# A hybrid attention/mLSTM layer step: the second head's scores moved next to the first head's transposes, and the first head's weighted values moved next to the second head's transposes

## What is computed

```python
q = (rmsnorm(cq_raw) @ w_q_up).reshape(B, T, 16, 128 + 64)      # per head: q_nope, q_pe
kv = (ckv @ w_kv_up).reshape(B, S, 16, 128 + 128)               # per head: k_nope, v
s = (q_nope . k_nope + q_pe . k_pe) * ATTN_SCALE                # scores
p = softmax(where(mask, s, -inf))                               # float32
out = p . v
```

## Time and profile before

| | us |
|---|---|
| median of 3 runs (lowest to highest) | 1999.95 (1999.67 to 2000.25) |
| the profiled execution | 1999.66 |
| its span, first to last instruction | 1997.9 |
| PE busy in the span | 1988.2 |
| DVE, ACT, POOL busy | 1211.7, 909.5, 192.3 |

### The profile page before, as it was taken

The page is one execution under the profiler, slowest core; times in us unless marked ns, Lnnn a source line. Parts: engine busy times, 40 slices in busy tenths (PEclk is TensorE's granted clock), DMA queues, the critical chain, the costliest instruction groups (busy, mean ns, idle before and its releaser), DMA issues.

```text
span 1997.9 us, 36175 instructions
## 1 busy us (share of the span) xinstructions
PE 1988.2 (100%) x14810; PEld 1963.9 (98%) x14810; DVE 1211.7 (61%) x2330; ACT 909.5 (46%) x1810; POOL 192.3 (10%) x228
## 2 busy tenths in 40 slices
PE   9999999999999999999999999999999999999998
PEld 9999999999999999999999999999999999999998
DVE  7856677676576576666765555444455665555554
ACT  5564455565444443434444444444444543333333
POOL 0011143434200000000000001000000000000000
PEclk9999999999999999999999999999999999999999
DMA  9765434343464554645545655555656566666665
GB/s 250 202 187 150 116 117 119 97 117 112 127 175 137 158 159 128 179 127 173 157 139 170 170 169 166 169 170 169 174 169 170 170 184 193 193 193 193 193 193 142
DMA packets 219262, 323.24 MB, mean 162 GB/s; under 512 B 28240, under 2 KB 100264, under 8 KB 219096
## 3 DMA queue, kind: packets, MB, share of 16 engines
q1 hardware_dynamic: 215800, 317.71, 55.3%
q10 hardware_dynamic: 3296, 3.22, 0.5%
HBM read 310.06 MB, written 9.62 MB: 160 GB/s over the span
## 4 chain that ended last, share of the span: by engine, by line
PE 98%; SPq 1%; DMA 0%; DVE 0%; ACT 0%; issue 0%; ACTq 0%
PE bank L1847 30%; PE bank L1851 30%; PE bank L1850 30%; PE bank L2113 1%; PE bank L2083 1%; PE bank L2009 1%; PE bank L2012 1%; PE bank L2011 1%; PE bank L2185 0%; PE bank L2211 0%; PE bank L2079 0%; SPq L469 0%; PE bank L2080 0%; DMA raw<-in_w_in_dram 0%; DMA xt<-in_meta_tokens_dram 0%; PE bank L2238 0%
## 5 line engine op out<-in xcount | busy, mean ns | idle before, releaser
L1205 DVE TENSOR_TENSOR wlo<-raw,whi 128x512 fp32r<-128x512 f32 (+1 forms) x1256 | 812.9, 657 | 731.5 <-ACT whi L796 723.7
L1847 PE MATMUL bank<-xsplit,whi 128*128 128x288 f32 (+2 forms) x4128 | 1217.0, 295 | 3.7 <-DVE xsplit L1229 2.7
L1851 PE MATMUL bank<-xsplit,wlo 128*128 128x288 f32 (+2 forms) x4128 | 1211.5, 293 | 0.0
L1850 PE MATMUL bank<-xsplit,whi 128*128 128x288 f32 (+2 forms) x4128 | 1211.2, 293 | 0.0
L796 ACT CAST whi<-raw 128x512 fp32r<-128x512 f32 (+1 forms) x1256 | 706.7, 576 | 957.7 <-PE bank L1851 915.3
L1847 PEld LDWEIGHTS bank<-xsplit,whi 128*128 128x128 f32 (+1 forms) x4128 | 772.6, 187 | 6.9 <-issue 5.1
L1850 PEld LDWEIGHTS bank<-xsplit,whi 128*128 128x128 f32 (+1 forms) x4128 | 772.6, 187 | 1.9 <-issue 1.0
L1851 PEld LDWEIGHTS bank<-xsplit,wlo 128*128 128x128 f32 (+1 forms) x4128 | 772.1, 187 | 0.0
L1847 PE MATMUL bank<-latents,whi 128*128 128x288 f32 (+1 forms) x352 | 112.7, 320 | 0.1
L1850 PE MATMUL bank<-latents,whi 128*128 128x288 f32 (+1 forms) x352 | 106.9, 304 | 0.0
L1851 PE MATMUL bank<-latents,wlo 128*128 128x288 f32 (+1 forms) x352 | 106.7, 303 | 0.0
(11 more groups left out here) (303 smaller groups left out, 1229.5 us busy)
## 6 DMA issues: line engine op xcount, KB each, us to landing
raw<-in_w_in_dram SPq DMA_DIRECT2D x313, 512.0 KB, 3.8
raw<-in_w_out_dram SPq DMA_DIRECT2D x128, 512.0 KB, 3.9
raw<-in_w_in_dram SPq DMA_DIRECT2D x142, 256.0 KB, 3.1
raw<-in_w_q_up_dram SPq DMA_DIRECT2D x48, 384.0 KB, 3.3
raw<-in_w_kv_up_dram SPq DMA_DIRECT2D x16, 512.0 KB, 3.6
xres<-in_x_prompt_dram SPq DMA_DIRECT2D x32, 128.0 KB, 3.9
xt<-in_x_prompt_dram SPq DMA_DIRECT2D x28, 128.0 KB, 5.1
out_dram<-ytok SPq DMA_DIRECT2D x28, 128.0 KB, 3.5
```

The source lines that it names most:

```text
L1205: ins = tt(lo, src, hi.bitcast(f32), ALU.subtract)
L1847: ins = mm(out, w_hi, m_hi, start=start, stop=False, **kw)
L1850: mm(out, w_hi, m_lo, start=False, stop=False, **kw)
L1851: return mm(out, w_lo, m_hi, start=False, stop=stop, **kw)
```

## The change

On PE, the second head's scores go from place 8 to place 9, so that they stand directly ahead of the first head's transposes. The first head's weighted values go from place 11 to place 12, directly ahead of the second head's transposes. On DVE, the second head's maxima follow the scores from place 8 to place 9. ACT, POOL and SP have the same lists as before. Nothing is computed otherwise.

```diff
@@ DVE, attention hooks @@
-                    if k == 8:
+                    if k == 9:
                         maxima(phase, i, j, 1)
                     if k == 10:
                         pt_minor(phase, i, j, 0)
@@ PE, attention hooks @@
                     if k == 5:
                         scores(phase, i, j, 0)
-                    if k == 8:
+                    if k == 9:
                         scores(phase, i, j, 1)
-                    if k == 9:
                         transposes(phase, i, j, 0)
-                    if k == 11:
+                    if k == 12:
                         weighted(phase, i, j, 0)
-                    if k == 12:
                         transposes(phase, i, j, 1)
                     if k == 13:
                         weighted(phase, i, j, 1)
```

## The result

| | before | after |
|---|---|---|
| median of 15 runs, us | 1999.95 | 2004.17 |
| lowest to highest, us | 1999.37 to 2001.66 | 2003.37 to 2006.57 |
| profiled execution, us | 1999.66 | 2003.45 |
| its span, us | 1997.9 | 2001.7 |

The ratio is 1.0020 with a 95% interval of 1.0013 to 1.0027: 4.2 us slower, against the 2.4 forecast (2002.3) and just outside the range's upper end of 2003.8.

A forecast was written before the change was run, and what follows sets the result against it. PE, busy for the whole span, was taken as the bound. Scores joins -0.1, weighted values 0 and unit 12's stalls +2.5 gave +2.4 us on the 1999.95 median: 2002.3, range 1999.3 to 2003.8.

The forecast's parts named there:

- the moved maxima: DVE's second-head maxima come 1.17 us later, covered by about 0.49 us before the exponentials, costing nothing; late-maxima rival 0.07.
- the transposes' start does not move: First head's transposes after the moved scores: start at 346.03 instead of 346.04, with POOL's scaling done at 345.92.
- the sum's 2.4: Whole kernel: -0.1 at the scores, 0 at the weighted values, +2.5 from unit 12's stalls, +2.4 us.
- Unit 12's gap: PE in unit 12 waits for DVE's copy of bank 0: 0.32 or 0.37 us in seven steps, 2.5 in all.
- The first pair: Unit 12 directly behind unit 11: PE resumes 0.06 after the copy, loses 0.10 restarting, 0.34 us in all.
- The joins: Float32 groups put directly before transposes: 0.01 us saved each at scores, 0 at weighted values; rival that they pay, 0.11.
- far from 1.5: Upper end for the weighted-values join, if its gap were a price of changing work: eight times 0.19, 1.5 us.

The follow-up runs named there:

- scores only: The changed kernel with the weighted values back at place 11, scores and maxima staying at place 9; median 2001.27 us.
- control: The kernel before with only DVE's copies of the queries moved ahead of its subtraction for unit 14; median 2000.09 us.
- weighted, copies early: The kernel before with weighted values moved to place 12 and DVE's query copies ahead of the subtraction for unit 14; median 1999.61 us.
- both fixes: The changed kernel with DVE's query copies ahead of the subtraction for unit 14 and the second head's maxima back at place 8; median 2000.05 us.
- copies early: The changed kernel with DVE's copies of the queries moved ahead of its subtraction for unit 14; median 2001.07 us.
- weighted only: The changed kernel with the second head's scores and maxima back at place 8, weighted values staying at place 12; median 2003.47 us.

## Why the prediction was wrong

**The step that failed** is the one on the moved maxima, "so this delay has cover of about 0.49 us and costs nothing", with the statement ahead of it that the transposes' start does not move, because POOL ends at 345.92 and PE asks at 346.04. The maxima themselves had their cover: the second one ended at 347.56 and the exponentials began at 348.12. But the row of POOL was taken as a constant. Moving the maxima also moves what DVE does in the meantime, and the subtraction for unit 12 slid under the start of POOL's third scaling: 0.16 us more, against a margin of some 0.06 us (0.12 less the 0.06 that a signal takes, as between 347.07, the end of POOL's scaling, and 347.12, the transpose). That the subtraction also overlapped this scaling in the kernel before, at no cost, because it came second, the prediction did not see. In five steps the transposes come 0.15 late. In pairs 0 and 4, where PE already lost 0.13 before, 0.44. That is 5 x 0.15 + 2 x 0.44 = 1.6 us, 1.4 of it new at these two distances; some of it is made up right behind them. From the start of unit 6 to the start of unit 11 the seven steps take 59.99 us in sum before and 61.07 after, so 1.1 us are lost. With the sum's 2.4 that makes 3.5.

**Unit 12's gap** was right in place, cause and nearly in size: 0.385 us in each of seven steps, 2.7 in all, against 0.32 and 0.37, 2.5 in all. The copy ended 4.00 us after the transposes' start instead of 3.94: the exponentials did start 0.04 after the end of the last transpose, but the transposes took 0.06 longer, having themselves waited. The first pair was a good model: 0.06 from the copy to PE, 0.10 for the restart.

**The joins** saved little, as said. At the scores nothing shows. At the weighted values, the weight loads of the changed kernel follow on as reckoned:

```profile
354.39 0.22 PEld L2094 LDWEIGHTS bank<-con,prob 128*128 128x128 f32 x1
354.53 0.14 PEld L2095 LDWEIGHTS bank<-con,prob 128*128 128x128 f32 x1
```

The last record starts at 354.39, the second transpose at 354.64. That is 0.26, against 0.19 + 0.11 = 0.30 if the transpose stood exactly where the main product did: 0.05 saved per pair, 0.4 us in eight, not nothing and far from 1.5.

**A term that was not in the sum.** The products of values (256 columns) run at two speeds, 0.115 or 0.122 us in the mean of a unit of twelve. The difference lies in the first eight of the twelve (0.113, or mostly 0.121 and 0.126 in turn); the last four take 0.115 to 0.12 in either case. Before, unit 12 was fast in all seven steps and unit 13 in three; after, unit 12 is slow in all seven and unit 13 too (the rows from 351.87 on show 0.12). Ten units more at 12 x 0.007 = 0.084 are 0.8 us.

The terms add to 2.7 + 1.1 + 0.8 - 0.4 = 4.2; the stretch grew by 4.07. The range missed by 0.4 us because it held only one of three losses. It took both others: with POOL's term alone the account gives 1999.95 + 3.4 = 2003.4, still inside the range, and what carried the time beyond 2003.8 is in part a term whose cause is not known.

What sets the speed of the value products was not settled. In unit 12 it was fast wherever the weighted values stood ahead of it (before, scores only, control), slow in nearly all steps of the kernels with a gap, and mixed where neither was so: in "weighted, copies early" slow in six of seven, in "both fixes" and "copies early" in two, with the same order on PE around unit 12. So the gap is not needed for it. In unit 12 of the first pair, ahead of which all nine kernels issue the same operations, it was fast in three traces (scores only, weighted only, both fixes) and slow in six, so there something other than the edits decides. These speeds make "weighted, copies early" 0.7 us slower than the control and, with 0.4 saved at the joins, give about its 0.24. They also account for the 0.6 us that "weighted only" took beyond what was expected. But their own cause is open, and with one trace of each kernel it is not shown that they belong to the kernel and not to the execution.

## What to carry to other kernels

Where one engine does everything and never waits, count for each moved operation what it covered, not only what it costs; 1.2 us of float32 products were the room in which bank 0 was emptied. And when an order on VectorE changes, read what GpSimd does beside it: a duration of POOL taken from a trace holds only while the same operations of DVE start before it and after it, and a margin below the size of that change is no margin.

## What the runs showed of the hardware that was not expected

POOL's scaling of 32 x 192 takes 0.75 us undisturbed. If a two-input subtraction of DVE is under way when it begins, with 0.17, 0.29 or 0.37 us left, it takes 0.80, 0.91 or 1.00 us. A subtraction that begins 0.12 us or 0.44 us after POOL's start costs POOL nothing. The one that began at 0.12 (pair 7 of the kernel before) took 0.83 us itself, the one at 0.44 took 0.67, against 0.69 with POOL idle.

A dense stream of products of 256 columns has two speeds on PE at the full granted clock, 0.115 and 0.122 us in the mean of a unit of twelve; the difference lies in the unit's first eight products.
